# A two-model fp32 kernel whose second mixer is reordered: decays first, recurrence levels and attention heads spread over the projection tiles

## The reference

```python
proj = x @ w_in                                     # 256 x 1024 by 1024 x 4608
da_q, da_k, da_v, hg_q, hg_ff, hg_fb, hg_i, hg_g, mx_q = split(proj)
# differential attention, 4 heads: a = softmax(q0 k0) - lam * softmax(q1 k1); da_o = a @ da_v, rms_norm
# hgrn2, 4 heads, chunks of 64, forwards and backwards:
hq  = silu(hg_q)
g_f = log(max(lb_f + (1 - lb_f) * sigmoid(hg_ff), 1e-20))    # the decays; g_b likewise from hg_fb
#   k = 1 - exp(g), b = cumsum(g) in a chunk, attn[t,s] = sum_k q[t] k[s] exp(b[t] - b[s]) for s <= t
#   state = exp(b_last) state + (k exp(b_last - b))^T v;  o = (q exp(b)) state + attn v
hg_o = rms_norm(o_fwd + o_bwd) * silu(hg_g)
# memory attention, 4 heads over 256 memory rows: softmax(mx_q mk / sqrt(128)) mv
mix = concatenate([da_o, hg_o, mx_o]) @ w_out       # 256 x 1536 by 1536 x 1024
x = layer_norm(alpha * x + mix)
```

## Time and profile before

| | before |
|---|---|
| median of three runs | 2422.75 us |
| profiled execution | 2425.84 us |
| its span | 2424.0 us |
| TensorE busy | 2132.1 us, 88% |
| VectorE busy | 1633.0 us, 67% |
| ScalarE busy | 1089.4 us, 45% |
| GpSimd busy | 334.2 us, 14% |
| second mixer, layer 0, first tile to tail | 1445.96 to 1708.19 us |
| second mixer, layer 1, first tile to tail | 1932.33 to 2194.18 us |

### The profile page before, as it was taken

One profiled execution on the slowest core, in us unless ns is written; L12 is line 12 of the kernel. 1 busy time (PEld: TensorE's weight loads), 2 busy tenths in 40 slices (PEclk: granted clock), 3 DMA queues, 4 the chain that ended last, 5 costly groups with the idle time before them and its releaser, 6 DMA issues. The chain is left out here.

```text
span 2424.0 us, 35482 instructions
## 1 busy us (share of the span) xinstructions
PE 2132.1 (88%) x14804; PEld 1970.7 (81%) x14804; DVE 1633.0 (67%) x2205; ACT 1089.4 (45%) x1529; POOL 334.2 (14%) x279
## 2 busy tenths in 40 slices
PE   6999889978998999899899967967799979677998
PEld 6999779968988997789789857956699779556996
DVE  6777677558777676776476554863787558747884
ACT  3443453434434444633354334642465446434652
POOL 0000303012002000231120001520300015203000
PEclk9999999979999999999899978978899989888999
DMA  9878532126785675431245524411255434122452
GB/s 374 308 278 325 187 144 96 61 88 241 283 318 198 258 266 195 166 109 53 70 183 226 208 105 159 159 50 52 88 182 194 163 142 157 53 70 87 174 185 111
DMA packets 59792, 409.98 MB, mean 169 GB/s; under 512 B 6832, under 2 KB 6832, under 8 KB 12912
## 3 DMA queue, kind: packets, MB, share of 16 engines
q1 hardware_dynamic: 53424, 384.85, 43.3%
q0 software_dynamic: 5920, 22.43, 2.4%
q10 hardware_dynamic: 288, 0.42, 0.0%
HBM read 404.53 MB, written 3.15 MB: 168 GB/s over the span
## 5 line engine op out<-in xcount | busy, mean ns | idle before, releaser
L578 DVE TENSOR_TENSOR l<-w,h 128x2048 fp32r<-128x2048 f32 (+1 forms) x296 | 689.7, 2334 | 247.6 <-ACT h L563 232.1
L682 PE MATMUL ps<-xh,h 128*128 128x256 f32 x2688 | 783.1, 291 | 74.5 <-DVE l L578 30.1
L683 PE MATMUL ps<-xl,h 128*128 128x256 f32 x2688 | 769.4, 286 | 0.0
L684 PE MATMUL ps<-xh,l 128*128 128x256 f32 x2688 | 768.4, 286 | 0.0
L563 ACT CAST h<-w 128x2048 fp32r<-128x2048 f32 (+1 forms) x296 | 558.4, 1891 | 318.9 <-PE ps L712 172.6
L682 PEld LDWEIGHTS ps<-xh,h 128*128 128x128 f32 x2688 | 524.4, 195 | 93.4 <-DVE l L578 31.4
L683 PEld LDWEIGHTS ps<-xl,h 128*128 128x128 f32 x2688 | 524.6, 195 | 1.9 <-issue 1.9
L684 PEld LDWEIGHTS ps<-xh,l 128*128 128x128 f32 x2688 | 524.4, 195 | 0.0
L710 PE MATMUL ps<-h,hh 128*128 128x512 f32 x528 | 207.7, 393 | 0.0
L712 PE MATMUL ps<-h,hl 128*128 128x512 f32 x528 | 205.8, 390 | 0.0
L711 PE MATMUL ps<-l,hh 128*128 128x512 f32 x528 | 205.7, 390 | 0.0
(11 more groups left out here) (408 smaller groups left out, 3103.2 us busy)
## 6 DMA issues: line engine op xcount, KB each, us to landing
w<-in_stream SPq DMA_DIRECT2D x362, 1024.0 KB, 4.8
GB<-in_vec POOLq DMA_DIRECT2D x20, 512.0 KB, 6.2
gate<-in_vec POOLq DMA_DIRECT2D x6, 512.0 KB, 4.0
w<-in_stream SPq DMA_DIRECT2D x6, 512.0 KB, 3.9
cst<-in_cst POOLq DMA_DIRECT2D x1, 1160.0 KB, 13.9
memf<-in_memT SPq DMA_DIRECT2D x1, 1024.0 KB, 8.7
xf<-in_xT POOLq DMA_DIRECT2D x1, 1024.0 KB, 9.7
kv<-mk POOLq DMA_DIRECT2D x2, 512.0 KB, 7.2
```

Of the source, the lines that this page charges most:

```text
L578: e.tensor_tensor(k.L[m % NH][:, 0:z], k.W[n % NW][:, 0:z], k.H[m % NH][:, 0:z], SUB).then_inc(k.lo_done, 1)
L682: p.matmul(P[:, 0:T], H[:, r, o], xh[:, r, :], start=r == 0, stop=False)
L683: p.matmul(P[:, 0:T], H[:, r, o], xl[:, r, :], start=False, stop=False)
L684: i = p.matmul(P[:, 0:T], L[:, r, o], xh[:, r, :], start=False, stop=r == 7)
```

## The change

The list is replaced. Chunks now go in the order `MIX2`: gates (four chunks), hgrn's queries, then differential attention's queries and keys, hgrn's values, differential attention's values, hgrn's gate, memory queries. `AFTER2` says which steps stand behind each tile: from tile 4 on hgrn's decays, from tile 11 two hgrn steps to a tile, which puts the six levels behind tiles 11 to 22, and from tile 19 differential attention's steps. Behind the last tile stand the closing transposes of both, then memory attention's five steps with the four output chunks between them.

Besides: the wait for GpSimd's `x` moves from the start of the stage to the first `KL`; `z` moves to a place that is free earlier; GpSimd adds `K` of both directions after the first differences, not before them; the meets stand one level later; `silu` of the queries and of the gate is done once over 1024 columns and no longer in each of the tiles' copies; the state products go by step and not by direction; the scaling of differential attention's first softmax moves from VectorE (two instructions a head, L2798) to the copy of its output (eight 128-column instructions in place of two of 512); output chunks are taken in the order of the heads.

```diff
+MIX2 = [2, 3, 4, 5, 0, 1, 6, 7, 8, 9, 12, 13, 10, 11, 14, 15, 16, 17]
-WOUT2 = [0, 1, 4, 5, 2, 3]
+WOUT2 = [0, 1, 2, 3, 4, 5]
...
+AFTER2 = ["", "", "", "", "h", "h", "h", "", "h", "h", "h", "hh", "hh", "hh", "hh", "hh", "hh", "hh", "hh", "hhd", "hhd", "hhd", "hhd", "hd",
+          "hd", "hd", "hd", "h", "hd", "hd", "hd", "hd", "hd", "d", "hd", "hd"]
...
     for t in range(36):
-        out.append(("tile", t // 2, t % 2))
-        if t >= 20 and t % 4 == 3:
-            out.append(("d",))
-        elif t >= 12:
-            out.append(("h",))
-    out += [("h",), ("d",)] * 13
-    out += [("out", 0), ("out", 1)]
-    out += [("h",), ("e",)] * 5
-    out += [("out", 2), ("out", 3)]
-    out += [("h",)] * 14
+        out.append(("tile", MIX2[t // 2], t % 2))
+        out += [(x,) for x in AFTER2[t]]
+    out += [("d",), ("h",), ("e",), ("out", 0), ("e",), ("out", 1), ("e",), ("out", 2), ("e",), ("out", 3), ("e",)]
...
 def dve_bounds(k, v, l):
-    v.wait_ge(*k.lg(STAGES.index(("mix2", l, 0)) - 1, "x", 3))
-    if not l:
-        return
...
     for lv in range(6):
         z, x = 1 << lv, lv % 2
+        if lv:
+            meet(lv - 2)
         yield
         for d in range(2):
             v.wait_ge(*ha(l, f"x{lv}{d}"))
             if d == 0:
-                if lv == 1:
+                if lv == 0:
+                    v.wait_ge(*k.m2_out(l, "qs"))
+                    v.wait_ge(*k.lg(STAGES.index(("mix2", l, 0)) - 1, "x", 3))
...
 def pool_hgrn(k, g, l):
-    g.wait_ge(*hv_(l, "K1"))
-    g.tensor_tensor(wide(k.KL[1][:, :, :]), wide(k.K2[:, 0, :, :]), wide(k.K2[:, 1, :, :]), ADD).then_inc(s, 1)
...
+            if lv == 0 and d == 0:
+                g.wait_ge(*hv_(l, "K1"))
+                g.tensor_tensor(wide(k.KL[1][:, :, :]), wide(k.K2[:, 0, :, :]), wide(k.K2[:, 1, :, :]), ADD).then_inc(s, 1)
...
-        v.tensor_scalar(m1[:, 0:2], m1[:, 6:8], lm[:, 5:6], None, MUL).then_inc(s, 1)
+        v.scalar_tensor_tensor(out=m1[:, 0:2], in0=m1[:, 6:8], scalar=lm[:, 5:6], in1=m0[:, 4:6], op0=MUL, op1=MUL).then_inc(s, 1)
         for a in range(2):
-            v.tensor_scalar(pp[:, x, 0, a, :], pp[:, x, 0, a, :], m0[:, 6 + a:7 + a], None, MUL).then_inc(s, 1)
...
-    for a in range(2):
-        e.copy(k.do[:, a, :], k.ps[(7, 3)[a]][:, :]).then_inc(s, 1)
+    for a in range(2):
+        for h in range(4):
+            c = slice(h * 128, h * 128 + 128)
+            e.activation(k.do[:, a, c], k.ps[(7, 3)[a]][:, c], ACT.Identity, scale=k.dmx[:, 2 * h, 6 + a:7 + a]).then_inc(s, 1)
...
-            e.activation(k.qs[:, i, :], P[:, 0:T], ACT.Silu).then_inc(o, 1)
+            e.copy(k.qs[:, i, :], P[:, 0:T]).then_inc(o, 1)
...
+        if (n, j) == (1, 1):
+            e.wait_ge(*k.m2_out(l, "c1", 1))
+            e.activation(k.qs[:, :, :], k.qs[:, :, :], ACT.Silu).then_inc(o, 1)
```

More of the change, by code:

```diff
@@ L104, in stage_chunks @@
     if kind == "mix2":
-        return [("win2", l, n) for n in range(18)] + [("wout2", l, k) for k in WOUT2]
+        return [("win2", l, n) for n in MIX2] + [("wout2", l, k) for k in WOUT2]
     if kind == "ffn2":
@@ L2292, in mixer2_steps @@
     for l in range(2):
-        k.m2_out.add(l, tile=36)
+        k.m2_out.add(l, **{f"c{n}": 2 for n in MIX2[:6]}, qs=1, **{f"c{n}": 2 for n in MIX2[6:16]}, hg=1, **{f"c{n}": 2 for n in MIX2[16:]})
         if l:
@@ L2386, in pe_hgrn @@
         yield
-    yield
     for lv in range(6):
@@ L2403, in pe_hgrn @@
     yield
-    for _ in range(4):
-        yield
+    yield
+    yield
     for d in range(2):
@@ L2414, in pe_hgrn @@
         yield
-    for d in range(2):
-        for i in range(3):
+    for i in range(3):
+        for d in range(2):
             n = i if d == 0 else 3 - i
             a, o = n // 2, 64 * (n % 2)
-            b = 4 + (3 * d + i) % 2
-            P = take(k, p, b)
+            P = take(k, p, 4 + d)
             if i == 0:
                 p.wait_ge(*ha(l, "kt", 2 * d + 1))
-                p.wait_ge(*k.m2_out(l, "tile", 27))
+                p.wait_ge(*k.m2_out(l, "c13", 1))
             for h in range(4):
@@ L2482, in dve_bounds @@
         v.tensor_scalar(z[:, d, 5, :], z[:, d, 4, :], -1.0, 1.0, MUL, ADD).then_inc(s, 1)
+    yield
 def act_bounds(k, e, l):
-    for d in range(2 * l):
+    for d in range(2):
         e.wait_ge(*k.hv_(l, "lbA", 3 * d + 2))
@@ L2524, in dve_hgrn, with meet @@
         yield
-    yield
+    def meet(n):
+        if n < 0:
+            v.wait_ge(*hg_(l, "A"))
+            dve_meet(k, v, l, "mD", k.ident)
+        else:
+            v.wait_ge(*hv_(l, "mD" if n == 0 else f"m{n - 1}", 1))
+            dve_meet(k, v, l, f"m{n}", k.both[:, n * 128:n * 128 + 128])
     for lv in range(6):
         z, x = 1 << lv, lv % 2
+        if lv:
+            meet(lv - 2)
         yield
@@ L2541, in dve_hgrn @@
             yield
-        if lv == 0:
-            v.wait_ge(*hg_(l, "A"))
-            dve_meet(k, v, l, "mD", k.ident)
-        else:
-            v.wait_ge(*hv_(l, "mD" if lv == 1 else f"m{lv - 2}", 1))
-            dve_meet(k, v, l, f"m{lv - 1}", k.both[:, (lv - 1) * 128:lv * 128])
-        yield
-    v.wait_ge(*hv_(l, "m4", 1))
-    dve_meet(k, v, l, "m5", k.both[:, 5 * 128:6 * 128])
+        yield
+    meet(4)
+    yield
+    meet(5)
+    for d in range(2):
+        b, end = chunks(k.B2[:, d, :, :]), 63 if d == 0 else 0
+        v.tensor_tensor(chunks(k.E[:, d, :, :]), b[:, :, end:end + 1].to_broadcast([128, 16, 64]), b, SUB).then_inc(s, 1)
     yield
@@ L2627, in act_hgrn @@
     for d in range(2):
-        e.wait_ge(*hp(l, "st", 3 * d))
-        e.copy(k.ST[3 * d][:, :], k.ps[4 + 3 * d % 2][:, :]).then_inc(s, 1)
-        for _ in range(3):
-            yield
+        e.wait_ge(*hp(l, "st", d))
+        e.copy(k.ST[3 * d][:, :], k.ps[4 + d][:, :]).then_inc(s, 1)
+    yield
+    yield
+    yield
     for a in range(2):
@@ L2720, in pe_diff @@
     yield
-    p.wait_ge(*k.m2_out(l, "tile", 23))
+    p.wait_ge(*k.m2_out(l, "c11", 1))
     out = [take(k, p, 7), take(k, p, 3)]
@@ L2996, in tile @@
         H, L = got["h"], got["l"]
-        r = x_in if n == 0 and j == 0 else None
+        r = x_in if n == MIX2[0] and j == 0 else None
         if n < 6 or n >= 16:
@@ L3050, in dve_mix2 @@
     cs = downs(s)
-    dve_bounds(k, v, l)
+    bounds = dve_bounds(k, v, l) if l else iter(())
+    next(bounds, None)
     def tile(n, j):
@@ L3055, in tile @@
         feed.lo(m + 1 + j)
+        if (n, j) == (MIX2[0], 1):
+            next(bounds, None)
     play2(tile, lambda c: feed.lo(cs[c] + 2), h=dve_hgrn(k, v, l), d=dve_diff(k, v, l), e=dve_memory(k, v, l))
```

111 lines of the change are left out of this document (59 added, 52 removed).

## The result

The changed kernel takes 2340.2 us (median of four runs, 2338.0 to 2341.0), the kernel before 2422.1 (2417.7 to 2423.3): a ratio of 0.966, 95% interval 0.965 to 0.968. That is 82 us less, where 60 were forecast (2362, range 2315 to 2403). The time lies inside the range, between the forecast and rival A (2327).

A forecast was written before the change was run, and what follows sets the result against it. Taken as bound by chains across engines behind the tiles; 172.7 us to the last tile, 14.8 closing and 44.5 for the end give 232 against 262.2, 30 less in each of two stages: 2362 us, range 2315 to 2403.

The forecast's parts named there:

- rival A: Tiles hide nearly all: levels keep TensorE's pace (11.5 us gone), closing wait covered (6.2 gone); 2327 us, chance 0.18.
- The start: Ahead of the first tiles, TensorE's gaps of 12.0 us (layer 0) and 15.1 us (layer 1) go; called nearly certain.
- TensorE's work up to the last tile: Layer 0's tiles, meets, attention heads, transposes, state products and outputs at 2.4 GHz durations: 148.2 us.
- Waits up to the last tile: TensorE's waits between tiles: 24.5 us, of which 11.5 over five levels at 9.9 us a level.
- The strict sum of 10.6 us: A level if VectorE and GpSimd never overlap, plus 0.5 us: 7 us more a stage, kernel 2376 us.
- Between the last tile and the first output chunk: Closing piece: wait for `do` 6.2 us, then 5.5 and 3.1 for transposes to products, 14.8 us in all.
- Output chunks and memory attention: Stage's end, interleaved: four chunks 24.8 us plus memory attention 19.7, together 44.5 us against 56.0 before.
- Edits costed at nothing: Eight 128-column `do` copies and two fewer VectorE instructions a head: cost nothing beside tiles, 2 us a stage if uncovered.
- B: Levels keep the old pace of 13.8 us each, six costing 23 us more a stage; 2409 us, chance 0.14.
- C: ScalarE's tile copies stuck behind chains, 3.0 us for each of 24 tiles from tile 12; 2457 us, chance 0.07.
- D: The gain at the start is returned by half of C: no change in time, chance 0.03.
- wrong if: Forecast fails if the tile stretch is under 155 or over 190 us, or pieces behind it miss 59 by over 8.

The follow-up runs named there:

- experiment 1: Kernel before, with only VectorE's wait for the last `x` moved from the stage's start to the first level's products (`z` moves too): 2388.1 us, ratio 0.986.
- experiment 7: Changed kernel with the transposes behind the rotation and all later differential attention steps one tile later: 2342.0 us, ratio 0.967.
- experiments 5 and 10: On the changed kernel, half of GpSimd's differences in levels 1 to 5: left out (5), 2319.4 us; given to VectorE (10), 2343.6 us.
- experiment 2: Changed kernel with VectorE's wait for the last `x` put back at the stage's start: 2355.9 us, ratio 0.973.
- Experiment 3: Changed kernel with memory attention's five steps ahead of the four output chunks, not between them: 2361.1 us, ratio 0.975.
- experiment 6: Changed kernel with differential attention's first softmax scaled on VectorE again and `do` copied in two instructions: 2338.1 us, ratio 0.965.

## Why the prediction was right, point by point

- **The start** (12.0 and 15.1 us gone): right in that neither stage has the gap any more, and VectorE's low parts follow ScalarE's. The step left out that the tiles behind the gap ran at a low clock, 3.4 us in layer 0 (experiment 1), and did not say that this term overlaps with the others (34 us alone, 15.5 undone). It also held that VectorE has nothing else to do before tile 4, and that the small instructions of the bounds in layer 1 lie beside the first tiles at no cost. They stand beside GpSimd's `x` as well, and there they do cost. One of them, and the product that waits for the low part behind them:

```profile
1893.87 2.38 DVE L2466 TENSOR_TENSOR z<-z 128x4 f32<-128x4 f32 x1
```

```profile
1906.99 0.39 PE L683 MATMUL ps<-xh,h 128*128 128x256 f32 x1 [1.97 <-DVE l L579]
```

Four times one or two such instructions took 2.26 to 2.38 us, where others took 0.15 to 0.24. With the decays late by them, TensorE then waits 4.0 us for a tile's copy behind the `Ln` step. So layer 1 did not gain as much as layer 0.
- **TensorE's work up to the last tile,** 148.2 us: 150.0 measured, 149.4 in layer 1.
- **Waits up to the last tile,** 24.5 us: the term that was mis-sized. TensorE was idle for 15.3 us in layer 0 and 18.7 in layer 1. The level was put at 9.9 us and took 8.4 to 8.6, so the levels' waits were 3.3 us. The forecast had 11.5. The work of the rotation on VectorE was in no term, and its 5.0 us of wait (experiment 7) make up for part of the error: by luck the sum of both, 8.3, is nearer.
  - The path was not the one named either: TensorE was to wait for ScalarE's late copies of tiles, and it waits for VectorE's meet, which empties the bank of the level before; of the waits from the levels on, one of 1.3 us was for a tile's copy.
  - The size 9.9 came from scaling a level by 0.89, the share that a mixed stretch took of its sum. The runs put a rule in its place: of a level's four differences three delay one instruction of VectorE each by some 0.85 us, and the fourth runs beside the copies from PSUM (experiments 5 and 10). In the stretch of the earlier trace rows all four level products took 1.52 to 1.53 us for 0.68 and both low parts were as short as alone, so there each of the four differences delayed one product: 6.8 us from start to start, as in the last level above, plus four times 0.85 are its 10.2. It holds no copy from PSUM, so its share could not be carried over to a level, and it was not better than the strict rule because some of VectorE's instructions don't compete. The strict sum of 10.6 us was wrong not in the lock but in counting the copies and the fourth difference as competing, and in adding durations (6.4 us) where starts are 5.85 us apart.
  - The first level was put at 4 us and cost 1.3, ScalarE late with a tile's copy. The `Ln` steps were put at 2 and cost 2.8 and 4.0; in layer 0 the cause was VectorE's decays beside GpSimd's `x`, without which the wait is gone (experiment 2). The attention heads were put at 4 and cost 2.7.
- **Between the last tile and the first output chunk,** 14.8 us: 10.8 (up to memory attention's first product, from which on the forecast counts with the next term). The wait for `do` was 3.7 and not 6.2. It was put down to GpSimd, where differential attention's norm stands behind hgrn's. But GpSimd was done at 1610.3, and VectorE, busy without a break from 1606.11 with a low part and the scaling of `ho`, came to `do` only at 1610.73.
- **Output chunks and memory attention,** 44.5 us: 44.0 from memory attention's first product, with the three waits of 1.8 and four of 0.7 named. Experiment 3 shows that 6 of the 11 us won here are clock.
- **Edits costed at nothing:** shown for the scaling (experiment 6). That `silu` over whole buffers, state products by step and meets one level later cost nothing was not tried alone.
- **Sum:** 42 and 37 us a stage for 30. Of the 12 us more in layer 0, 7.3 lie in the tiles, 4.0 behind them, 0.5 in the closing piece. The forecast was too high in each of the three; within the tiles two errors partly cancel. The 2340.2 lie nearer to A's 2327 than to the forecast's 2362.
- **Rivals.** A went part of the way: of its 11.5 us for the levels 3.2 came, of its 6.2 for `do` 2.5. The level keeps VectorE's pace, not TensorE's. B's 13.8 us a level did not come. C needed 2.3 us of wait a tile behind tiles 12 to 35; there were 12.3 us in all, and one of them, 1.3 us, was for a tile's copy. D: no.
- **Signs and readings.** The level products stood 8.4 to 8.6 us apart, neither the forecast's 9 to 11 nor A's 7.6. Of the level products on VectorE two in each level took 1.3 to 1.5 us and two 0.7, where most were to take 1.5. In the stretch behind the tiles before, the other engines were not all busy less than half the time: VectorE was 70 of 131.9 us, 53%.
- The bounds of "wrong if" held: a tile stretch of 165 and 168 us (155 to 190), and 54.8 us behind it against 59.

How the remaining 48 us (82 less the 34 of the start alone) divide is settled only in part: undoing memory attention's interleaving costs 21, the tiles' order nothing, and since parts overlap (experiment 2) such numbers need not add. That the rest is the levels and heads spread over the tiles is argued by exclusion, not shown; a kernel that spreads them and leaves the start and memory attention as before was not run.

## What to carry to other kernels

Price work between VectorE and GpSimd by who starts first: look in both timelines for which instruction holds the other up, and time GpSimd's work so that it comes second behind a long instruction of VectorE and then runs beside its copies from PSUM. A wait that appears in front of one product may be the arrears of an engine that is the bound; moving the product moves the wait, so relieve the engine. When short chains are put between large products, count the clock as well as the idle time: in experiment 3 it was 6.2 of 11.3 us.

## What the runs showed that was not expected

- A small operation can wait as long as the large one beside it. GpSimd's scaling of 128x4 numbers, 0.19 us for the half before, took 2.19 us when it started 0.15 us into a low part of VectorE, and ended with it. It did not lengthen the wait for `do`, since VectorE was busy until later. In layer 1 the same befell small instructions of VectorE beside GpSimd's `x` (above). Timeline of GpSimd, then of VectorE, changed kernel:

```profile
1606.26 2.19 POOL L3098 TENSOR_SCALAR dms<-dms 128x4 f32<-128x4 f32 x1
```

```profile
1606.11 2.29 DVE L579 TENSOR_TENSOR l<-w,h 128x2048 fp32r<-128x2048 f32 x1 [1.04 <-ACT h L564]
```

- The same products cost TensorE 5.0 us less busy time when VectorE kept up (experiment 5), at a granted clock of 0.97 for 0.94 over the tiles, and 6.2 more when memory attention stood alone (experiment 3), at 0.75 for 0.92.
